# A merge stage's first loads and the pooled products moved into the attention's last rows, its lower parts in another order, and eight identity products ahead of PE's first merge unit

## The reference, cut to what matters

```python
def pool_mix(p, w_grp, scale):            # 4 groups of 64 channels, windows 2, 4, 8, 16
    d = centred_mean(g, w) - g            # per group
    return einsum('btgc,gcd->btgd', d, w_grp) * scale      # then times silu(gate)

def merge_branches(branches, merge_logits, w_br, w_out):
    gates = sigmoid(merge_logits)
    y = gates[..., :D] * (branches[0] @ w_br[0])
    for i in range(1, 4):
        y = y + gates[..., i*D:(i+1)*D] * (branches[i] @ w_br[i])
    return y @ w_out
# x = x + gate * merge_branches([gm, na, rw, pl], ...); out = rmsnorm(x, final_g)
```

## Time and profile before

| | |
|---|---|
| median of 3 runs | 2583.83 us (2577.88 to 2587.68) |
| profiled execution | 2572.3 us, of which the span is 2570.6 us |
| PE busy | 2270.5 us, 88% of the span |
| DVE busy | 1560.4 us, 61% |
| ACT busy | 1015.1 us, 39% |
| POOL busy | 188.5 us, 7% |
| mean granted TensorE clock | 0.953 of full speed |

### The profile page before, as it was taken

How to read it: one execution, slowest core, us unless ns; L and a number is a source line. 1 busy time by engine, 2 the same in 40 slices (tenths; PEclk the granted TensorE clock), 3 DMA queues, 4 the chain that set the end, 5 groups by cost and what they waited for, 6 DMA issues and landing times. The chain is left out here.

```text
span 2570.6 us, 65138 instructions
## 1 busy us (share of the span) xinstructions
PE 2270.5 (88%) x26434; PEld 1854.1 (72%) x26434; DVE 1560.4 (61%) x2583; ACT 1015.1 (39%) x1739; POOL 188.5 (7%) x260
## 2 busy tenths in 40 slices
PE   4999999999899999999668787778695797799998
PEld 2788878888688878888556676667565575677787
DVE  5756656667755456666366666666363577756744
ACT  5454234444522124444345444545323665311111
POOL 0000000000000000000120010000032650000000
PEclk7999999999999999999879999999797899899999
DMA  6343333332333233333321111110356521734542
GB/s 229 110 135 115 108 113 99 112 115 98 119 99 106 88 102 108 110 118 103 92 57 35 34 43 34 35 34 20 115 191 201 134 92 51 278 123 164 197 140 89
DMA packets 253116, 279.50 MB, mean 109 GB/s; under 512 B 34411, under 2 KB 177899, under 8 KB 250347
## 3 DMA queue, kind: packets, MB, share of 16 engines
q1 hardware_dynamic: 250602, 267.94, 32.7%
q10 hardware_dynamic: 2304, 8.39, 0.8%
HBM read 184.66 MB, written 91.62 MB: 107 GB/s over the span
## 5 line engine op out<-in xcount | busy, mean ns | idle before, releaser
L715 PE MATMUL proj_ps<-h_hi,w_hi 128*128 128x512 f32 x1656 | 650.0, 393 | 28.8 <-DVE h_lo L465 20.8
L716 PE MATMUL proj_ps<-h_lo,w_hi 128*128 128x512 f32 x1656 | 646.9, 391 | 0.0
L717 PE MATMUL proj_ps<-h_hi,w_lo 128*128 128x512 f32 x1656 | 646.6, 390 | 0.0
L318 ACT CAST w_hi<-w_raw 128x512 fp32r<-128x512 f32 x420 | 255.1, 621 | 695.8 <-PE proj_ps L717 353.1
L715 PEld LDWEIGHTS proj_ps<-h_hi,w_hi 128*128 128x128 f32 x1656 | 312.5, 189 | 99.1 <-issue 27.7
L717 PEld LDWEIGHTS proj_ps<-h_hi,w_lo 128*128 128x128 f32 x1656 | 312.2, 189 | 65.7
L716 PEld LDWEIGHTS proj_ps<-h_lo,w_hi 128*128 128x128 f32 x1656 | 312.7, 189 | 63.5
L482 DVE TENSOR_TENSOR w_lo<-w_raw,w_hi 128x512 fp32r<-128x512 f32 x420 | 283.1, 688 | 44.2 <-ACT w_hi L318 43.8
L498 DVE TENSOR_TENSOR z_slots<-proj_ps,x_rows 128x512 f32<-128x512 f32 x174 | 120.2, 691 | 171.1 <-PE proj_ps L717 169.0
L498 DVE TENSOR_TENSOR x_rows<-proj_ps,x_rows 128x512 f32<-128x512 f32 x116 | 80.2, 691 | 109.7 <-PE proj_ps L717 103.7
L2647 PE MATMUL late_ps<-mb_hi,mw_hi 128*128 128x512 f32 x256 | 102.5, 400 | 26.3 <-DVE mb_lo L2554 19.3
(11 more groups left out here) (343 smaller groups left out, 3934.1 us busy)
## 6 DMA issues: line engine op xcount, KB each, us to landing
w_raw<-in_w_in SPq DMA_DIRECT2D x240, 256.0 KB, 3.0
scratch_gatesT<-z_slots SPq DMA_DIRECT2D x128, 256.0 KB, 2.7
m_gate<-scratch_gatesT SPq DMA_DIRECT2D x64, 512.0 KB, 3.9
scratch_zT<-z_slots SPq DMA_DIRECT2D x108, 256.0 KB, 2.4
ada<-in_ada_w SPq DMA_DIRECT2D x4, 2048.0 KB, 15.2
mb_rows<-scratch_branchT SPq DMA_DIRECT2D x16, 512.0 KB, 4.8
x_res<-in_x SPq DMA_DIRECT2D x16, 512.0 KB, 4.6
out<-x_res ACTq DMA_DIRECT2D x16, 512.0 KB, 2.6
```

The costliest lines, as they stand in the source:

```text
L318: A.copy(wh[:, i, :, :], raw[:, q, :, :]).then_inc(w_hi, 1)
L715: T.matmul(out, wh[:, i, k, :], hi[:, o, k, :], start=(first and k == 0), stop=False, skip_group_check=not first)
L716: T.matmul(out, wh[:, i, k, :], lo[:, o, k, :], start=False, stop=False, skip_group_check=not first)
L717: last = T.matmul(out, wl[:, i, k, :], hi[:, o, k, :], start=False, stop=(k == 3), skip_group_check=not first)
```

## The change

SP issues seven of the merge's first loads inside the attention block, after the scores of row 31 and the eighth scaled weight block, and before it waits for the last gate. For that the merge's gate, branch-row and weight tiles are placed over `q_t`, `k_t`, `v_t` and a part of `na_gate`, and the semaphores live above both blocks. SP waits for the stores' landing at the start of the merge block in place of the attention block's end; DVE waits there for the attention's stores before its first `multiply`. The other weights are loaded in halves of 512 KB by columns, and those of branches 1 follow the wait. The pooled products of blocks 0 and 1 go into PE's steps 32 and 33, ahead of the output transposes of rows 30 and 31. ACT's SiLU of the pooled gate is in four pieces. The lower parts of the weights of branch 1 come after units 1 and 3, those of later branches after units 0 and 2, and the lower part of the branch rows after unit 1 in branches 1 and 2 of every block (after unit 2 in branch 0). PE begins the merge block with eight 128x128 products of the identity with itself, in plain f32.

```diff
@@ attention_stage, SP @@
+                if end == ROWS:
+                    fp.after(sp, ROWS - 1, "S")
+                    sp.wait_ge(scaled, KT)
+                    load_merge_w(sp, t, s, 0, 0)
+                    load_merge_rows(sp, t, s, 0, 0)
+                    load_merge_gate(sp, t, s, 0, 0, 0)
+                    load_merge_gate(sp, t, s, 0, 0, 1)
+                    load_merge_w(sp, t, s, 0, 1)
+                    load_merge_gate(sp, t, s, 0, 0, 2)
+                    load_merge_gate(sp, t, s, 0, 0, 3)
                 bvg.after(sp, end - 1, "g")
...
-            sp.wait_ge(stored, 64 * len(PARTS))
-            sp.wait_ge(pl_stored, 16 * NB)
@@ attention_stage, ACT @@
-            A.activation(pg, pg, ACT.Silu).then_inc(pl_silu, 1)
+            for b in range(NB):
+                c = slice(b * BLK, (b + 1) * BLK)
+                A.activation(pg[:, :, c], pg[:, :, c], ACT.Silu).then_inc(pl_silu, 1)
@@ attention_stage, PE @@
+            def pool_products(b):
+                if b == 0:
+                    pe.wait_ge(diff_set, 2)
+                    pe.wait_ge(plw_in, 16 * 5)
+                    fv.after(pe, ROWS - 1, "b1")
+                if b >= 2:
+                    pe.wait_ge(pl_out, b - 1)
+                for p in range(2):
+                    last = T.matmul(ps[:, 2 * (b % 2) + p, :], plw[:, p, :], dd[:, p, b * BLK:(b + 1) * BLK], start=True, stop=True)
+                last.then_inc(pl_ps, 1)
...
                 if valid(n - 1):
                     turn_probs(n - 1)
+                if n >= ROWS and n < ROWS + 2:
+                    pool_products(n - ROWS)
                 if valid(n - 2):
                     bvr.after(pe, n - 2, "o")
                     bot.done(T.transpose(ps[:, 7, BR:BR + P], on[:], s["ident"][:]), "OT")
-            bvg.after(pe, ROWS - 1, "g")
...
+            pool_products(2)
+            pool_products(3)
@@ merge_and_output_stage, SP @@
+            sp.wait_ge(s["na_stored"], 64 * 3)
+            sp.wait_ge(s["pl_stored"], 16 * NB)
+            load_merge_w(sp, t, s, 1, 0)
+            load_merge_rows(sp, t, s, 0, 1)
+            load_merge_w(sp, t, s, 1, 1)
...
-                        if n == 0 and i < 2 and p == 1:
-                            load_w(i + 2)
+                        if n == 0 and i < 2 and p in (1, 2):
+                            load_merge_w(sp, t, s, i + 2, p - 1)
@@ merge_and_output_stage, ACT @@
             split_w(1, 0)
+            split_b(0, 1)
             split_w(1, 1)
-            split_b(0, 1)
...
@@ merge_and_output_stage, DVE @@
             split_w(0, 1)
+            dve.wait_ge(s["na_stored"], 64 * 3)
...
-                        if n == 0 and i < 3 and p < 2:
-                            split_w(i + 1, p)
-                        if p == 2 and (i < 3 if n == 0 else i in (1, 2)):
+                        if n == 0 and i < 3 and p in ((0, 2) if i else (1, 3)):
+                            split_w(i + 1, 0 if p < 2 else 1)
+                        if p == (1 if i else 2) and (i < 3 if n == 0 else i in (1, 2)):
                             split_b(n, i + 1)
@@ merge_and_output_stage, PE @@
+            for k in range(8):
+                T.matmul(ps[:, 3, 0, 0:P], s["ident"][:], s["ident"][:], start=True, stop=True)
             def unit(n, i, p):
-                if n == 0 and (i == 0 and p % 2 == 0 or p == 0):
-                    pe.wait_ge(w_l, 2 * i + 2 if i else p // 2 + 1)
+                if n == 0 and p % 2 == 0:
+                    pe.wait_ge(w_l, 2 * i + p // 2 + 1)
```

More of the change, by code:

```diff
@@ L2397, in split @@
             return rows, sb(f"{name}_hi", shape, F32R), lo
+        gate, br, w = s["merge_gate"], s["merge_rows"], s["merge_w"]
+        sb("m_gate_place", [P, 4, 2, BLK])
+        b_lo, w_lo = sb("mb_lo", [P, 2, 2, BLK], F32R), sb("mw_lo", [P, 4, 2, D], F32R)
+        y, y_hi, y_lo = split("y", [P, KT, BLK])
+        b_hi, w_hi = sb("mb_hi", [P, 2, 2, BLK], F32R), sb("mw_hi", [P, 4, 2, D], F32R)
         wo, wo_lo = s["wo_rows"][:, 0:KT * D].rearrange("p (k n) -> p k n", k=KT), s["wo_lo"]
         wo_hi = sb("wo_hi", [P, KT, D], F32R)
[L2400 to L2403, removed]
         xr, fg = sb("x_res", [P, 2, D]), sb("final_g_rows", [P, D])
@@ L2480, in split_w @@
             def split_w(i, h):
-                act.wait_ge(w_in[4 if (i, h) == (0, 1) else i], 16)
+                act.wait_ge(w_in[i][h], 16)
                 A.copy(w_part(w_hi, i, h), w_part(w, i, h)).then_inc(w_h, 1)
@@ L2714, in late_stages, with load_merge_gate, load_merge_rows, load_merge_w @@
         s["wo_lo"] = ctx.enter_context(nc.sbuf_tensor("wo_lo", [P, KT, D], F32R))
-        with ExitStack() as edges:
-            edges.enter_context(nc.sbuf_tensor("wo_rows_end", [P, 8 * EDGE], F32))
-            s["wo_in"] = ctx.enter_context(nc.semaphore("wo_in"))
-            attention_stage(nc, t, s)
-        merge_and_output_stage(nc, t, s)
+        ctx.enter_context(nc.sbuf_tensor("wo_rows_end", [P, 8 * EDGE], F32))
+        with ExitStack() as under:
+            s["merge_gate"] = under.enter_context(nc.sbuf_tensor("m_gate", [P, 4, 2, BLK], F32))
+            s["merge_rows"] = under.enter_context(nc.sbuf_tensor("mb_rows", [P, 2, 2, BLK], F32))
+            s["merge_w"] = under.enter_context(nc.sbuf_tensor("mw_rows", [P, 4, 2, D], F32))
+        s["wo_in"] = sem("wo_in")
+        s["gate_in"] = [[sem(f"gate_in{p}{par}") for par in range(2)] for p in range(4)]
+        s["rows_in"] = [sem("b_in0"), sem("b_in1")]
+        s["w_in"] = [[sem(f"w_in{i}{h}") for h in range(2)] for i in range(4)]
+        s["na_stored"], s["pl_stored"] = sem("na_stored"), sem("pool_stored")
+        attention_stage(nc, t, s)
+        merge_and_output_stage(nc, t, s)
+def load_merge_gate(sp, t, s, n, i, p):
+    src = t["gatesT"][8 * i + 2 * p:8 * i + 2 * p + 2, :, n * BLK:(n + 1) * BLK]
+    sp.dma_start(s["merge_gate"][:, p, :, :], src.rearrange("m p t -> p m t")).then_inc(s["gate_in"][p][i % 2], 16)
+def load_merge_rows(sp, t, s, n, i):
+    src = t["branchT"][2 * i:2 * i + 2, :, n * BLK:(n + 1) * BLK]
+    sp.dma_start(s["merge_rows"][:, i % 2, :, :], src.rearrange("m p t -> p m t")).then_inc(s["rows_in"][i % 2], 16)
+def load_merge_w(sp, t, s, i, h):
+    src = t["w_br"].rearrange("l i (k p) n -> p (l i) k n", p=P)[:, i, :, h * BLK:(h + 1) * BLK]
+    sp.dma_start(s["merge_w"][:, i, :, h * BLK:(h + 1) * BLK], src).then_inc(s["w_in"][i][h], 16)
 STAGES = (front_stage, recurrence_stage, late_stages)
```

49 lines of the change are left out of this document (12 added, 37 removed).

## The result

The changed kernel took 2552.44 us (median of 4 executions, 2549.63 to 2555.99) beside 2583.5 us for the one before (4 executions, 2577.88 to 2587.68): ratio 0.9882, 95% interval 0.9857 to 0.9907. The two profiled executions differ by less: spans of 2570.6 and 2548.0 us, 22.6 apart. So the sum, which was made against the profiled execution, agrees with the profile and not with the medians. What follows first checks the sum row by row, then looks for the other 9 us.

What follows compares the result with a forecast made beforehand. At the seam no engine was the bound but a store landing, block change and load flight; afterwards PE or DVE. Gains 6.9 + 2.6 + 1.9 + 3.3 + 0.3 + 7.0 = 22.0 us gave 2561.8 us, range 2555 to 2572.

Steps and rivals of the forecast that it cites:

- the sum: All gains from the attention's last rows to the end added up: 22.0 us, taking the profiled execution from 2572.3 to 2550.3.
- The seam: Between attention and merge: store landing and load flight leave the path, first unit at 2185.5 instead of 2192.36, 6.9 us gained.
- The clock at the first unit: Merge start on PE: identity products split the pause, so full clock was taken, 2.6 us gained, bounds 0 and 2.6.
- the 1.9 us put down to order: Token block 0, first unit to branch 1's first `multiply`: 4.5 us gained, 2.6 of it clock, 1.9 the new order.
- Token block 0: Merge's first token block: DVE becomes the bound; branch 1 to branch 3 takes 26.0 instead of 29.3, 3.3 us gained.
- the first rival: PE starts the merge at the half clock, so the 2.6 us are not gained: 2564.4 us, chance 0.19.
- Weights in halves: Merge weight loads of 512 KB instead of 1024 KB: costed at nothing, landings of 6.4 and 6.6 us.
- Token blocks 1 to 3: Later merge blocks: earlier lower part of the rows removes six PE waits, 7.3 less 0.3, so 7.0 us gained.
- The level: Whole kernel: profiled execution was 11.5 us faster than the 2583.83 median; the same microseconds taken off that median give 2561.8.
- Late upper parts: Rival, merge: casts come too late for the new order and its gains go, 2574.0 us, chance 0.10.
- stretched rows: Rival, attention's last rows: loads or pooled products slow them, seam gives back up to 6.9 us, 2568.7, chance 0.05.
- DVE's wait for the stores: Rival, merge start: attention stores land late and hold DVE's merge, slower than before, 2588 us, chance 0.04.

Runs made afterwards that it cites:

- x2: The changed kernel run again without an edit: 2556.53 us, ratio to before 0.9912.
- x14: The changed kernel run again without an edit, its third profile: 2548.33 us, ratio to before 0.9903.
- x4: The changed kernel without the eight identity products on PE: 2554.58 us, ratio to before 0.9898.
- x6: The changed kernel with its seven early loads issued at the start of the merge block: 2559.41 us, ratio to before 0.9934.
- x3: The kernel before with one edit, the branch rows' lower part after unit 1 in token blocks 1 to 3: 2567.74 us, ratio 0.9953.
- x7: The changed kernel with token block 0's old order of lower and upper parts on DVE and ACT: 2555.99 us, ratio to before 0.9908.
- x1: The kernel before, run again without an edit: 2577.87 us, ratio to before 0.9995.
- x13: The kernel before, run again without an edit for a third profile: 2570.05 us, ratio to before 0.9989.
- x9: The changed kernel with DVE's pooled output of block 0 ahead of the last gate: 2556.19 us in one execution.
- x10: The changed kernel with the first pooled product halved into two PE pauses and block 1's products behind the last transpose: 2558.49 us in one execution.
- x11: x10 with, in token block 0, one more lower part of weights in branch 0 and one less in branch 2: 2549.19 us, ratio to before 0.9908.
- x8: The changed kernel with GpSimd in place of DVE making the lower weight parts of branches 1 to 3: 2552.79 us, ratio to before 0.9905.

## Why the prediction was wrong, point by point

**The seam** was right: last gate, last output, block change and first unit within 0.1 us. That the pooled products moved forward gain nothing was right in its mechanism and 0.6 us off in size: the right comparison is products last without the wait for the gate, which is 0.8 us better.

**The clock at the first unit** came out as forecast in the changed kernel, three profiles of three, but not for the reason given. "Nearest is the longer of them, under 2.71, so I take full clock" failed: in x2 and x14 the clock fell behind a pause of 2.35 us and was back only 0.3 and 0.4 us before the first unit, which is luck. The 2.6 us are mis-sized too. In the kernel before, branch 1 waited for its load and started at the same time whatever the clock at the first unit, so nothing was there to gain; in the changed kernel, without the identity products, it cost 1.4 us (x4), and 1.6 in x6, where the loads were late as well. The total up to branch 1, 4.5 us behind the first unit, was right all the same, because the 1.9 us put down to order were too few: the landing of branch 1's weights left the path as well. Order, halves and loads were not told apart there.

**Token block 0** from branch 1 on is a term that one execution mis-sized. "From branch 1 to branch 3 are 26.0 in place of 29.3: 3.3 us" holds for that execution of before, and for x3. In the other two profiles the clock fell behind each of the three pauses, and they lose 3.0 us more: 1.3 and 1.6 up to `multiply` of branch 1, 1.1 from there to that of branch 3, the rest behind it. The rows that I used for the first rival, the fall behind a pause of 2.71 us, stood in that same stretch; I priced them for the first unit and not for the pauses that the new order removes. x7 shows them at work: 1.8 us of order and 1.3 of clock.

**Weights in halves** were "costed at nothing", from 512 KB landing in 6.4 us and 1024 KB in 6.6 "in the same crowd of loads". It was not the same crowd: the 6.6 is the median of three, and the one of them issued in the crowd took 13.2 us. What halves alone are worth was not tried.

**Token blocks 1 to 3**: the mechanism was right, the size 8.1 us and not 7.0 (x3). The 0.3 that I took off for late `multiply`s did not show, and a wait costs 1.35. What makes up the last 0.1 of each was not looked for.

Against the first profile of before, the gain from the eighth scaled block on is 23.2 us, of which 0.6 are lost in the span because that block came 0.6 later. Against x1 and x13 it is 22.0 + 3.0 + 1.1 = 26.1 us by the corrected sum, and 26.0 to 26.2 by the profiles. How many executions lose the 3.0 is not known; it was two of the four profiles with the old order in token block 0. The comparisons of x2 and x14 gave 23 and 26 us.

**The level** is the step that put the result outside the range. "I take the same microseconds off that median" used a median of 3 executions as if it were known, and the range allowed some 4 us for it. The same kernel before had medians of 2583.5, 2579.2, 2576.9, 2573.5 and 2574.5 in five sessions, so the level of 2583.83 lay 5 to 10 us above those of the four later sessions, and the two kernels' own medians move apart from each other. The 5 to 8 us by which the first comparison, 31, exceeds 23 to 26 I take to be such a draw; that is argued and not shown. Its interval, 0.9857 to 0.9907, does hold the 0.9903 of x14, but not the 0.9912 of x2. Whether chips differ or only executions was not told apart, nor what makes the spread in the shared code; the mean granted clock goes with the time only in part (in x1 2571.09 us at 0.960, 2588.22 at 0.955, but 2572.85 at 0.955 too).

**Rivals.** Half clock at the first unit did not come about in the changed kernel, but did in each of x9, x10 and x11, with a tail 1.7 to 2.1 us shorter. Late upper parts, stretched rows and DVE's wait for the stores did not come about in any run of the changed kernel.

## What to carry to other kernels

A pause of PE of two to three microseconds had two prices here, its length and a stretch of half clock that followed in some executions: behind 9 of the 12 pauses of 2.5 to 3.1 us between branches, in before, x1, x13, x3 and x7, at some 1.1 us each between branches 1 and 3. One profile shows only one draw of the second, so price an edit that removes such pauses with both ends. Before you price a slow stretch, ask what opened the next step: where a load did, the faster engine would only have waited longer. What is moved off the path at a seam is the flight of the first loads; moving products ahead of work that the last step waits for only swaps one wait for another. And a forecast in microseconds is worth no more than the level it stands on: count from a point behind the shared code, and widen the range by the draw of both medians.

## What the runs showed of the hardware that was not expected

A DVE subtraction of 128x1024 took up to 3.43 us in place of 1.22 while GpSimd did the same operation (x8), and GpSimd's 2.4 us became 3.2; a DVE instruction with an operand in PSUM kept its 1.2 us. Six subtractions handed over made the kernel's part no faster. The same code brought DVE to the eighth scaled weight block at anything between 2157.7 and 2172.9 us in 16 profiled executions, while the 388 us behind it repeated within 0.2 in the three of the changed kernel. And with the attention's tail 1.7 to 2.1 us shorter the first units met the half clock in three runs of three, with the identity products in place (2.62 to 2.83 us for them instead of 2.02). There the fall came 1.0 to 1.3 us behind the first identity product and lasted 6.8 us; with the longer tail it came within 0.3 us of that product and lasted 3.4 us (x2, x7, x8 and x14), or did not come (the first profile). That the shorter tail is the cause is not shown: it is one profile of each version.
